# Latent attention: for its first three head pairs TensorE makes a pair's scores ahead of the next pair's turning, not behind it

## The reference

```python
def multi_head_latent_attention(h, positions, w_in, q_norm, w_uq, kv_norm, w_ukv, w_out):
    ...
    scale = 1.0 / math.sqrt(MLA_NOPE_DIM + MLA_ROPE_DIM)
    k_idx = jnp.arange(s)
    def block(args):
        qb, bi = args
        q_idx = bi * Q_BLOCK + jnp.arange(Q_BLOCK)
        qn, qr = qb[..., :MLA_NOPE_DIM], qb[..., MLA_NOPE_DIM:]
        scores = (jnp.einsum('bqhd,bkhd->bhqk', qn, k_nope)
                  + jnp.einsum('bqhr,bkr->bhqk', qr, k_rope)).astype(jnp.float32) * scale
        mask = k_idx[None, :] <= q_idx[:, None]
        scores = jnp.where(mask, scores, -jnp.inf)
        p = jax.nn.softmax(scores, axis=-1).astype(v.dtype)
        return jnp.einsum('bhqk,bkhd->bqhd', p, v)
    ...
    return merge_blocks(o) @ w_out
```

## Time and profile before

| | before |
|---|---|
| median of 3 runs | 2719.38 us (2717.86 to 2719.91) |
| time of the profiled execution | 2720.06 us |
| its span, first to last instruction | 2718.3 us |
| mean granted clock of TensorE, share of full | 0.967 |
| PE, DVE, ACT, POOL busy | 2452.0, 1910.9, 1180.0, 837.6 us |
| latent attention, first turning to last pair's values | about 753.6 to 803.8 us of the span |

### The profile page before, as it was taken

The page is one execution under the profiler, slowest core; times in us unless marked ns, Lnnn a source line. Parts: engine busy times, 40 slices in busy tenths (PEclk is TensorE's granted clock), DMA queues, the critical chain, the costliest instruction groups (busy, mean ns, idle before and its releaser), DMA issues.

```text
span 2718.3 us, 32050 instructions
## 1 busy us (share of the span) xinstructions
PE 2452.0 (90%) x10370; PEld 1669.7 (61%) x10370; DVE 1910.9 (70%) x3856; ACT 1180.0 (43%) x2587; POOL 837.6 (31%) x691
## 2 busy tenths in 40 slices
PE   8999999999999999998898787788988888788798
PEld 7887788888778887996444333234764444333344
DVE  6885588888768875665666767666667676776775
ACT  4446654444565447563333332333553333323333
POOL 0006300000220017764333333444133333333442
PEclk9999999999999999999999898999999999888899
DMA  6554355555525544448999999999649999999996
GB/s 204 189 178 140 123 191 185 178 193 187 172 72 193 185 164 139 163 156 339 420 418 421 417 420 417 414 414 419 222 174 420 421 419 420 412 421 416 414 416 261
DMA packets 142240, 783.39 MB, mean 288 GB/s; under 512 B 15904, under 2 KB 16416, under 8 KB 76576
## 3 DMA queue, kind: packets, MB, share of 16 engines
q0 software_dynamic: 73728, 536.90, 47.7%
q1 hardware_dynamic: 65648, 237.45, 25.9%
q10 hardware_dynamic: 2736, 7.46, 0.9%
HBM read 780.69 MB, written 1.05 MB: 288 GB/s over the span
## 4 chain that ended last, share of the span: by engine, by line
PE 42%; DMA 26%; DVE 7%; ACT 7%; issue 4%; POOL 3%; POOLq 0%; DVEq 0%; ACTq 0%
DMA arena<-experts,arena 26%; PE ps L717 8%; PE ps L695 6%; PE ps L696 6%; PE ps L697 6%; PE ps L1326 5%; PE ps L1329 5%; PE ps L718 4%; DVE arena L2782 3%; ACT row L1945 2%; POOL arena L2899 2%; ACT arena L1938 1%; ACT L1936 1%; POOL ring_lo L401 1%; DVE ring_lo L401 1%
## 5 line engine op out<-in xcount | busy, mean ns | idle before, releaser
L2782 DVE SCALAR_TENSOR_TENSOR arena<-arena,ps 128x1024 f32<-128x1024 f32 x512 | 617.2, 1219 | 382.6 <-DMA arena<-experts,arena 380.9
L1326 PE MATMUL ps<-arena,row 128*128 128x512 f32 x1024 | 570.4, 640 | 206.0 <-ACT row L1945 206.0
L2899 POOL DMA_INDIRECT arena<-experts,arena x512 | 483.4, 944 | 763.6 <-PE ps L1329 511.1
L1329 PE MATMUL ps<-arena,row 128*128 128x512 f32 x1024 | 551.4, 621 | 0.0
L717 PE MATMUL ps<-hT,ring_hi 128*128 128x512 f32 x1408 | 504.4, 401 | 3.9 <-DVE hT L2272 3.7
L394 ACT ACTIVATE ring_hi<-ring 128x1024 fp32r<-128x1024 f32 x408 | 429.4, 1058 | 173.1 <-PE ps L697 130.2
L1326 PEld LDWEIGHTS ps<-arena,row 128*128 128x128 f32 x1024 | 198.2, 202 | 484.9 <-ACT row L1945 279.7
L718 PE MATMUL ps<-hT,ring_lo 128*128 128x256 f32 x1408 | 396.3, 281 | 0.0
L401 POOL TENSOR_TENSOR ring_lo<-ring,ring_hi 128x1024 fp32r<-128x1024 f32 x130 | 317.9, 2455 | 232.8 <-ACT ring_hi L394 205.8
L1329 PEld LDWEIGHTS ps<-arena,row 128*128 128x128 f32 x1024 | 206.2, 201 | 267.7 <-issue 267.7
L401 DVE TENSOR_TENSOR ring_lo<-ring,ring_hi 128x1024 fp32r<-128x1024 f32 x278 | 334.7, 1228 | 18.8 <-ACT ring_hi L394 18.2
(11 more groups left out here) (350 smaller groups left out, 3562.3 us busy)
## 6 DMA issues: line engine op xcount, KB each, us to landing
ring<-stream SPq DMA_DIRECT2D x424, 512.0 KB, 3.4
arena<-experts,arena POOLq DMA_INDIRECT x512, 13.1
row<-rows_in ACTq DMA_DIRECT2D x11, 512.0 KB, 4.9
arena<-stream SPq DMA_DIRECT2D x8, 512.0 KB, 5.4
queries_in_ring_hi<-stream SPq DMA_DIRECT2D x8, 512.0 KB, 6.2
queries_in_w<-stream SPq DMA_DIRECT2D x4, 512.0 KB, 7.9
queries_in_h_lo<-stream SPq DMA_DIRECT2D x4, 512.0 KB, 4.8
x<-x_in SPq DMA_DIRECT2D x1, 1024.0 KB, 4.9
```

The costliest lines, as they stand in the source:

```text
L1326: lower = pe.matmul(ps[:, 2 * tb, :], diag, v[:, 0:HALF], start=first, stop=end)
L1329: pe.matmul(ps[:, 2 * tb + 1, :], diag, v[:, HALF:D], start=first, stop=end)\
L2782: last = dve.scalar_tensor_tensor(u, u, 1.0, h, ALU.mult, ALU.mult, accum_out=R["a"][:, n % 2, k:k + 1])
L2899: pool.indirect_dma_start(R["held"][:, g % HELD, :], None, experts, bass.IndirectOffsetOnAxis(ap=idx[:, n % 2, k:k + 1], axis=0))\
```

## The change

For `a` = 0 the loop ahead of the main loop runs `scores(j)` and then `turn_q(j + 1)`, for j = 0, 1 and 2; before it was `turn_q(j + 1)` and then `scores(j)`. For `a` = 1 nothing changes. No instruction is added or removed, and the other engines' lists stay as they are.

```diff
                 turn_q(0)
                 for j in range(3):
-                    turn_q(j + 1)
-                    scores(j)
+                    if a:
+                        turn_q(j + 1)
+                        scores(j)
+                    else:
+                        scores(j)
+                        turn_q(j + 1)
                 for j in range(pairs):
```

## The result

The changed kernel takes 2723.0 us (median of 20 runs, 2719.98 to 2725.96), the kernel before 2719.09 (20 runs, 2717.0 to 2720.17). The ratio is 1.0016, 95% interval 1.0009 to 1.0022: 4.35 us slower, between 2.4 and 6.0; the medians lie 3.9 us apart. The point forecast was 2722.6.

A forecast was written before the change was run, and what follows sets the result against it. Latent attention's end was taken to hang on when ScalarE's full stretch starts, handing over to TensorE at 782.39. Lateness of 2.32, then 3.17 us, gave 2719.38 + 3.2 = 2722.6 us; own range 2721.0 to 2724.5, 8 in 10 2719.3 to 2726.0.

The forecast's parts named there:

- The place: Latent attention: ScalarE's full stretch starts at exps(0), 763.21, and hands to TensorE at 782.39; a us there is one at the end.
- Steps 1 to 6: Start of latent attention to hand-over: changed order traced row by row; first exponential 2.32 us late, then lateness stays at 3.17.
- the sum: Whole kernel: 3.2 us of lateness added to the median 2719.38, giving 2722.6 us; chance 0.70.
- Step 2: VectorE, pair 0: masked(0) gets scores at 759.41 and runs from 759.55, 1.62 us earlier, with nothing gained.
- Nothing is gained by it: ScalarE: masked(0)'s 1.62 us earlier start gives nothing, because exps(0) has take_q(2) ahead of it.
- VectorE's head start: Rival at the first exponential: masked(0) 1.62 us earlier decides, about -1.6 us, 2717.8 in all; chance 0.05.
- the round's pace: Latent attention's start: copy j, scores j, turning j + 1, copy j + 1 form a ring the old order kept open.
- The clock rival: TensorE, start of latent attention: new 1.1 us gaps keep half clock for two pairs, +3.3 more, 2725.9; chance 0.10.
- the prediction's own signs of being wrong: First exponential near 761.6; lateness at 785.6 without a longer span; or granted clock below 1.00 from 762 to 768.
- the forecast's own range: Whole kernel: 2721.0 to 2724.5 us, for a missing 0.85, one slow pair, or scatter between runs.
- the range for 8 in 10: Whole kernel: 2719.3 to 2726.0 us, taking in absorption and the clock case, leaving out the head start.
- The absorption rival: Out-products from pair 4 on: held by something not late, such as POOL's low parts; no change, down to 2719.4; chance 0.12.

The follow-up runs named there:

- With the order turned round and the clock held: Changed kernel with exps(0), exps(1) ahead of copies 2, 3 on ScalarE, plus 9 unread products in TensorE's idle: stretch 29.93 us, time 1.0003 to before.
- the second or the third swap alone: Kernel before with only pair 1's, or only pair 2's, scores put ahead of the next turning: stretches 31.21 and 31.23 us, times 1.0008 and 1.0012.
- the three with one swap: Kernel before with scores ahead of the next turning for pair 0, 1 or 2 only: stretches 29.79, 31.21, 31.23 us; times 1.0006, 1.0008, 1.0012.
- the exponentials ahead: Changed kernel with exps(0) ahead of take_q(2) and exps(1) ahead of take_q(3) on ScalarE, no unread products: stretch 34.28 us, time 1.001.
- the new order with the products: Changed kernel plus 9 products nobody reads in TensorE's idle of 2.3 us: stretch 30.41 us, time 1.0001 to before.
- the old order with the table load moved: Kernel before with ScalarE's load of the exponentials' table behind its first copy in latent attention: stretch 25.95 us, time 0.9990.

## Why the prediction was right

*The place* held. ScalarE's full stretch started with the first exponentials, each us there was a us at the hand-over, and TensorE passed it on.

*Steps 1 to 6* held nearly to the row. All times of the profile after are 0.28 us early (756.70 for 756.98). With that added: copies of pairs 1, 2, 3 at 761.13, 764.70, 768.26 (forecast 761.07, 764.61, 768.15), first exponential of pairs 0 and 1 at 765.62 and 769.18 (765.53, 769.07), hand-over at 785.66 (785.56). The stretch grew by 3.27 where the sum said 3.17. Step 2 alone was off by half a us: VectorE got its scores at 760.04 and not at 759.55, because I took the length of scores whose last part ran when the clock had come back (2.43), and all of them ran at half clock here (756.70 to 759.61, 2.91). It lay on no path. All this is the first profile of the changed kernel.

*"Nothing is gained by it"* (VectorE's head start) was right in the number and short in the reason. I gave ScalarE's order as the cause. With the order turned round and the clock held, 2.79 of the 3.27 us stayed. The head start is worth little because the copies come at the round's pace, with the exponentials between them or not.

*The clock rival* was given 0.10, and it came in part. In two of three profiles of the changed kernel half clock held through one more pair. There one of the prediction's own signs of being wrong, a granted clock below 1.00 from 762 to 768, is met: in the second profile it is 0.50 until about 766.7. Its price was mis-sized: I took +3.3 for two pairs, at 1.63 each from a row that was only mostly at half clock. Measured, a pair of scores and turning almost wholly at half clock costs 2.1 more (4.57 against 2.45), only one such pair was hit, and the first was half a us longer: together 34.72 - 32.07 = 2.65. The stretch is then 5.9 over before. Its mechanism was off too: it blamed the new gaps of 1.1 us, and the profiles part before the first of them (last section).

So the 3.2 us of the sum belong to the executions in which the clock comes back early, and that the median fell 0.4 us from the forecast is in part luck. A median 3.9 over before, and a ratio that says 4.35, lie between 3.3 and 5.9, as they would if the executions are of both kinds. Only one execution of each set of timed runs has a profile, so the shares are not shown. The scatter of the times can't tell them either: it was 6.0 us against 3.2 in the first sets of 20, but the kernel before had 5.5 to 6.0 in its later sets of 27 to 33. Nor is it shown that the kernel before is free of it: it has one profile, and the two that start in its order, with the second or the third swap alone, had the clock back as early. The total stood within the forecast's own range and the range for 8 in 10.

*The absorption rival* fell at the hand-over: TensorE idles the same 0.32 us for ScalarE as in the earlier trace rows, 3.3 us later.

## What to carry to other kernels

Where two engines hand a single buffer to and fro, put into each wait the work that the other engine needs next; here a turning that was run inside the wait of the scores held up nothing, and behind them it set the pace of the round. Getting the first result of a pipeline earlier is worth little if the feeding of the next ones becomes slower (0.8 us earlier here, and a stretch 2.8 longer): price the round, not the first arrival. And look for what stands between two hand-overs with no need, such as a table load of 1.28 us ahead of the first copy.

## What the runs showed of the hardware

Half clock, once granted, was not left after the same time in every execution. It set in within 0.2 us of the end of the same idle of 2.31 us in all eight profiles that kept that idle. In five of them (before, the first profile of the changed kernel, the three with one swap) it lasted about 3.4 us, in three (the other two of the changed kernel, and the exponentials ahead) about 10.2. These are two stretches of the changed kernel's first profile and one of its third:

```profile
756.90:760.10 3.20, 3.20 (x12) 2.67 (x13) 0.34 (x1) 0.00 (x0) 0.00 (x0) 0.50 0.00 0
760.30:768.00 7.70, 5.42 (x37) 4.34 (x35) 4.14 (x9) 3.81 (x11) 0.00 (x0) 1.00 0.00 0
```

```profile
755.30:759.90 4.60, 4.60 (x16) 3.64 (x16) 1.50 (x3) 0.00 (x0) 0.00 (x0) 0.50 0.00 0
```

In the first the clock was back at 760.2, after 3.5 us of work without a gap. In the third it was still at half after 4.6 us of work without a gap (755.29 to 759.93), when the first gap of 1.11 us had not yet begun. So the two differ before the gap, and the gap can't be what parted them. Nor did such gaps bring a full clock down: it stayed at 1.00 through three of them in the new order with the products (751 to 768, TensorE busy 13.37 of 17.00 us), and through one in the old order with the table load moved. What decides between the short and the long case stays open: list and waits are the same in both. The Trainium skill's "TensorE: Matmul & The Clock Gate", The HAM clock gate, has the throttled state as the default and activity as what lifts it. The first profile agrees; the other two show that work without a gap did not always lift it at once.
